# Inside an attention unit: scores first and transposes last on TensorE, the exponential ahead of the copy on ScalarE

## The reference, cut to what matters

```python
q = heads(pr['nsa_q'])                                  # 8 heads of 64, 2 key groups
o_cmp, imp = _nsa_compressed(q, pos, k_c, v_c)          # 31 compressed keys
o_sel = _nsa_sel_attend(rope(q), pos, kg, vg, kpos)     # chosen blocks: with 512 positions, all
o_win = _window_attend(rope(q), pos, k, v, kpos)        # window of 512: all earlier positions
no = gate[..., 0] * o_cmp + gate[..., 1] * o_sel + gate[..., 2] * o_win
# each branch: p = exp(s - max(s)) / sum, under a causal mask;  o = p @ v
```

## Time and profile before

| | |
|---|---|
| median of 3 runs | 2518.5 us (2511.68 to 2520.64) |
| the profiled execution | 2515.68 us, its span 2514.1 us |
| busy TensorE | 2198.9 us, 87% of the span |
| busy VectorE, ScalarE, GpSimd | 1259.0, 805.4, 418.5 us |
| joint stage, first layer | about 368.4 to 721 us of the span |
| joint stage, second layer | about 1617 to 1970 us |
| granted TensorE clock, mean over the span | 0.887 of full speed |

### The profile page before, as it was taken

The page is one execution under the profiler, slowest core; times in us unless marked ns, Lnnn a source line. Parts: engine busy times, 40 slices in busy tenths (PEclk is TensorE's granted clock), DMA queues, the critical chain, the costliest instruction groups (busy, mean ns, idle before and its releaser), DMA issues. The chain is left out here.

```text
span 2514.1 us, 36111 instructions
## 1 busy us (share of the span) xinstructions
PE 2198.9 (87%) x12280; PEld 1625.6 (65%) x12280; DVE 1259.0 (50%) x2982; ACT 805.4 (32%) x1678; POOL 418.5 (17%) x648
## 2 busy tenths in 40 slices
PE   6999868888889999997979997688788799999977
PEld 3644447667767887886346444477677588888853
DVE  2244364566536666654122534545664366666532
ACT  2211112334334444441222211133343345445402
POOL 0110001001133333420001100010111333344100
PEclk9999867889869999995979997688888799999969
DMA  4452100000066877862044521000000768678431
GB/s 180 161 193 67 46 22 2 1 10 1 1 152 161 185 175 155 189 128 82 32 146 161 184 67 37 23 1 1 10 1 2 176 164 182 159 177 185 101 113 38
DMA packets 173056, 243.10 MB, mean 97 GB/s; under 512 B 50714, under 2 KB 132282, under 8 KB 172192
## 3 DMA queue, kind: packets, MB, share of 16 engines
q1 hardware_dynamic: 143328, 147.27, 23.0%
q0 software_dynamic: 29536, 93.43, 14.4%
HBM read 223.69 MB, written 25.50 MB: 99 GB/s over the span
## 5 line engine op out<-in xcount | busy, mean ns | idle before, releaser
L609 PE MATMUL bank<-W,hT 128*128 128x512 f32 (+3 forms) x1152 | 447.7, 540 | 14.2 <-DMA W<-in_w_in 10.1
L609 PEld LDWEIGHTS bank<-W,hT 128*128 128x128 f32 x1152 | 216.6, 194 | 203.4 <-issue 172.1
L978 PE MATMUL bank<-XT,W 128*128 128x256 f32 (+1 forms) x768 | 250.8, 462 | 0.0
L1035 POOL DMA_DIRECT2D SHARED<-in_cache_nsa_kv x256 | 152.1, 594 | 454.0 <-DVE RP L948 353.9
L1219 POOL TENSOR_TENSOR work<-UP,SHARED 128x512 f32<-128x512 f32 x56 | 72.2, 1293 | 877.0 <-DVE UP L1504 518.5
L967 ACT ACTIVATE XT<-bank 128x512 f32<-128x512 f32 x256 | 140.1, 593 | 125.6 <-PE bank L960 124.7
L1035 POOL DMA_DIRECT2D PS<-in_cache_nsa_kv x256 | 150.7, 589 | 138.7 <-issue 126.5
L1428 DVE TENSOR_REDUCE mx<-bank 128x1 f32<-128x31 f32 (+4 forms) x192 | 75.0, 390 | 196.5 <-PE bank L1287 193.3
L978 PEld LDWEIGHTS bank<-XT,W 128*128 128x128 f32 x768 | 135.0, 190 | 49.6 <-issue 36.9
L960 PE MATMUL bank<-CF,RP 128*128 128x128 f32 x1024 | 146.2, 289 | 9.2 <-DVE RP L948 8.8
L1247 ACT ACTIVATE Pr<-bank,mx 128x31 f32<-128x31 f32 (+4 forms) x192 | 85.7, 446 | 210.3 <-DVE mx L1429 210.0
(11 more groups left out here) (395 smaller groups left out, 3732.8 us busy)
## 6 DMA issues: line engine op xcount, KB each, us to landing
SHARED<-in_cache_nsa_kv SPq DMA_DIRECT2D x256, 128.0 KB, 5.7
SHARED<-in_cache_nsa_kv POOLq DMA_DIRECT2D x256, 128.0 KB, 5.5
PS<-in_cache_nsa_kv SPq DMA_DIRECT2D x256, 128.0 KB, 6.2
PS<-in_cache_nsa_kv POOLq DMA_DIRECT2D x256, 128.0 KB, 5.8
W<-in_w_in SPq DMA_DIRECT2D x48, 512.0 KB, 3.8
XS<-scratch_conv_p POOLq DMA_DIRECT2D x24, 384.0 KB, 4.5
PW<-in_state_nsa_win SPq DMA_DIRECT2D x16, 512.0 KB, 3.8
Wo<-in_w_out SPq DMA_DIRECT2D x4, 2048.0 KB, 11.9
```

Of the source, the lines that this page charges most:

```text
L609: return nc.tensor.matmul(bk((c * NTILE + t) % BANKS)[:, 0:b - a], hT[:, k, t * P:(t + 1) * P], W[:, k // 2, k % 2, 0:b - a], start=(k == ...
L978: mm = nc_(self.v).tensor.matmul(out, self.v['W1'][:, kv, s, :], seg[:, s], start=(s == 0), stop=(s == SEG // PAIRS - 1))
L1035: e.dma_start(where[side * HD:(side + 1) * HD, slot, :, :], A['cache_nsa_kv'][l, page].rearrange("(p r) a g d -> p r (a g d)", r=PAIRS)[:, ...
```

## The change

Within an entry of the list, scores(u) go ahead of values(u-2) and transposes(u-1) on TensorE, and on ScalarE the exponential of u goes ahead of the group copy and of copy(u-1). All waits stay with their instructions. VectorE's code is as it was.

```diff
@@ block.scalar, unit(u)
+                if u < NU:
+                    qt, br, h = units[u]
+                    n = keys(u)
+                    e.wait_ge(shift, u + 1)
+                    if u >= DEEP:
+                        e.wait_ge(turned, u - DEEP + 1)
+                    nc.scalar.activation(Pr[:, u % DEEP, 0:n], sbank(u)[:, 0:n], ACT.Exp, scale=SCALE, bias=mx[:, u % DEEP, 1:2],
+                                         accum_out=SUM[:, u // GROUP % 2, h % 2, br:br + 1]).then_inc(exped, 1)
                 if u >= 2 and (u - 2) % GROUP == GROUP - 1:
                     k = (u - 2) // GROUP
                     e.wait_ge(used, u - 1)
...
                     nc.scalar.activation(PT[0:m, (u - 1) % 2, 0:k, :], bk(TURN, 4)[0:m, 0:k, :], ACT.Copy).then_inc(copied, 1)
-                if u < NU:
...
@@ block.tensor
                 if what == "unit":
+                    if x < NU:
+                        scores(x)
                     if x >= 2:
                         values(x - 2)
                     if 1 <= x <= NU:
                         turn(x - 1)
-                    if x < NU:
-                        scores(x)
                     continue
```

## The result

| | before | after |
|---|---|---|
| median | 2517.8 us (2511.7 to 2520.6, 4 runs) | 2492.2 us (2488.2 to 2495.7, 4 runs) |
| ratio | | 0.9903, interval 0.9881 to 0.9926 |
| span of the profiled execution, granted clock | 2514.1 us, 0.887 | 2486.6 us, 0.898 |
| joint stages, by TensorE's first product to that of the next stage | 353.9 and 354.4 us | 334.0 and 337.9 us |
| samples' attention, likewise | 456.5 and 452.3 us | 462.8 and 462.6 us |

The change made the kernel 1% faster. It gained 36 us in the joint stages, and 17 of them were given back in the two stages behind, whose code is the same. What else differs between the two spans (8 us) lies in stages that the change doesn't touch. The stages behind hold the same code in every kernel here (but for one run's filler) and took 451 to 463 us over all profiles, so the 17 us are what this pair of profiles shows, not a fixed price.

A forecast was written before the change was run, and what follows sets the result against it. It took the in-order hand-over of units between engines as the bound, the clock as second limit. Per layer -3.3 - 1.5 - 4 + 5 + 0 = -3.8 us, two layers -7.6 from 2515.7: 2508 us, range 2472 to 2536.

The forecast's parts named there:

- the forecast's own range: Whole kernel: 2496 to 2518 us, given a chance of 0.45.
- rival A: Joint stages: fewer gaps let TensorE keep 2.4 GHz, 26 us less, 2480 us (2465 to 2495); chance 0.20.
- Start: Joint stage's opening: scores(1) runs in the gap before transposes(0), gaining 3.3 us a layer, bounds 2.0 and 3.5.
- Tail: Units after the last delta steps: three small waits go, gaining 1.5 us a layer, bounds 0.5 and 2.5.
- the direct sum: Gains and prices at an unchanged clock: -3.8 us a layer, -7.6 for two layers.
- Middle: Units between the ends: half of 8.2 us of small transposes' waits goes, gaining 4 us a layer, bounds 0 and 8.2.
- The sign: First joint stage: if right, the transposes' wait for the exponential falls from 26.9 us to under 10.
- The slot's rule: One unit: exponential's way (L) plus copy (C) covered by values, transposes, delta step, scores (V+T+D+S); idle next to none.
- Price 1: Group ends, 16 a layer: VectorE's chain waits for the later group copy, costing about 5 us a layer, bounds 0 and 18.
- Price 2: Five norms a layer: copy runs behind table load and exponential, nearly cancelled by a wait gone; 0, bounds -3 and +5.
- rival B: Group ends: VectorE's stand-still decides, +9 us a layer, 2534 us (2527 to 2545); chance 0.22.

The follow-up runs named there:

- one run's filler: Kernel after plus 44 dummy products on TensorE in the gap before a page tile in the samples' attention: 2482.0 us, ratio 0.9873.
- The filler: Kernel before, order untouched, plus six dummy products per list entry from unit 87 on, ahead of the transposes' wait: 2502.4 us, ratio 0.9958.
- two edits: Kernel after with VectorE's group chain one entry later, or with ScalarE's group copy ahead of the exponential again: 2470.6 us and 2468.4 us.
- the filled start: Kernel before plus dummy products at both stage ends, 16 at unit 0, six at units 1 to 8 and 83 to 95: 2529.6 us, ratio 1.0048.
- the halves of the change: TensorE's new order alone against the kernel before: 2427.2 us; adding ScalarE's new order to that gives the kernel after: 2492 us.

## Why the prediction was right, and where not

The time, 2492, lies in the range and 16 us under the point of 2508; it lies outside the forecast's own range (from 2496), 3 us inside rival A's (2465 to 2495). For the forecast's own sum that is luck: it came near by two errors of opposite sign, and what moved the time is the rival's mechanism. By its steps:

- **Start, -3.3 a layer: right.** L1355 came 3.6 us sooner. Up to unit 6 the gain was 9.1 in this stage, the clock's part included.
- **Tail, -1.5: the waits went, but the size was wrong.** From unit 84 on the gain was 5.3 to 7.1 us over the six stages, beyond the bound of 2.5. The filler shows 4.7 us there to be the clock's, which the direct sum left out.
- **Middle, half of 8.2: too small on the transposes' side.** Their waits fell by 26.2 us, not by some 8. (The sign said "under 10"; the sum, with 14.6 us left to a late VectorE, could not give that.) The waits in which VectorE was late vanished from the transposes too, because values, now in front of them in the queue, wait first.
- **The slot's rule, "L+C must be covered by V+T+D+S", is the step that failed.** It took VectorE as free when scores are done. The rows at 514.21 and 514.94 show it in delta work: exp(u) waits for that, and copy(u-1) behind it. Values' waits came to 41.9 us for the 20 forecast, 32 of them with the maximum behind VectorE's own work. Of these, 18.9 us are nine waits of over 1.6, of which those for units 36, 42 and 78 stand at group ends.
- **Price 1, 5 us: too small.** L1435 waited 24.3 us, at all 16 group ends, and not at six; two edits that take 13 to 15 of it away gave 9 us a stage. The bounds (0 to 18) held it. The larger cost, some 18 us a stage for the copy behind the exponential, is no term of the sum: the slot's rule had put it at next to none.
- **Price 2, norms at 0: not shown as a whole.** Where norm and group end met, near 637 us, both table loads (the square root's at 635.36), the exponential and both copies stood ahead of the values:

```profile
637.45 1.28 ACT L1234 ACT_TABLE_LOAD   x1
638.75 0.58 ACT L1234 ACTIVATE Pr<-bank,mx 128x384 f32<-128x384 f32 x1
...
639.32 0.48 ACT L1241 ACTIVATE OB<-bank 128x384 f32<-128x384 f32 x1
639.69 0.49 ACT L1248 ACTIVATE PT<-bank 128x384 f32<-128x384 f32 x1
...
640.23 1.44 PE L1309 MATMUL bank<-UP,PT 128*128 128x64 f32 x6 [3.42 <-ACT PT L1248]
```

The exponential starts 0.02 us behind its load, as in the earlier trace rows; the drain that the Trainium skill ("ScalarE: Activation LUTs", "What ACT_TABLE_LOAD costs") adds to a switch doesn't show here either.

- **The direct sum, -3.8 a layer, came out at about 0:** TensorE's idle time changed by +1.3 and +1.9 us. The signs named for rival B were all there (idle time over 62 in the first stage, values at 41.9, L1435 at 24.3), but its longer time was not.
- **Rival A happened, given a chance of 0.20.** It gave 26 us for a quarter of the slow stretches turned fast (its point should read 2482: 2508 less 26). Of them 39 and 35 hundredths did, worth 39 us of products, and 17 came back in the samples' attention, which the sum did not have. Its sign, a clock over 0.87, came in the first stage (0.89) and stood at 0.87 in the second. "Against it: the long gaps stay" was true and not decisive, since the slow stretches that went lay mostly at the two ends. That it is the clock is shown for the tail, by the filler; why it rose sooner at the start is not shown. The Trainium skill says ("TensorE: Matmul & The Clock Gate", Part 1) that activity releases the throttle. The filled tail agrees; in the filled start it was not released soon, with 12 us of full TensorE at 0.50.

So the time was right with a gain and a cost that were both far too small: the terms of two layers were -17.6 and +10, the halves of the change measured -90 and +65.

## What to carry to other kernels

Before an instruction is put ahead in an in-order queue, ask when its input comes in the slot where the engine upstream is latest, not in the typical one. Here the exponential's input hung on another engine's long work while the copy's was ready, and the ready one belonged in front. Split a change that reorders two engines and time the halves: here one gained 3.6%, the other lost most of it again. And compute idle and busy time apart: a stage that got shorter with its idle time unchanged was paid by the clock, and varies with it from one profile to the next.

## What the hardware showed that was not expected

- Six small products a unit put a tail with gaps of 0.4 to 1.1 us at 2.4 GHz; without them it ran at 1.2 GHz though busy for 3.0 to 3.7 of each 4 us (692 to 716 us, before).
- Full occupation doesn't bring the clock back at once: 12 us at 0.50 in the filled start, and in the kernel after 17 us behind a 3.8 us gap, where in the kernel before it was 3.4 us behind one of 3.0.
- The same code ran 462.7 and 451.2 us in two layers of one execution, by the clock alone.
